# Group A attention: the products of a pair of query tiles issued in two halves, at other places of the TensorE order

## What is computed

```python
qa = _axial_rope(_rmsnorm(qa.reshape(b, s, N_Q_A, HEAD_DIM), q_norm_a[i]), tables)   # 8 query heads of 64
ka = _axial_rope(_rmsnorm(ka.reshape(b, s, N_KV_A, HEAD_DIM), k_norm_a[i]), tables)  # 2 key/value heads
sc = jnp.einsum('bqkgd,bskd->bkgqs', qblk, k) * scale      # scores of 128 queries against all keys
p = jax.nn.softmax(sc, axis=-1)
o = jnp.einsum('bkgqs,bskd->bqkgd', p, v)                  # "weighing" of the values
```

## Time and profile before

| | us |
|---|---|
| three runs, median | 2393.69 (2391.83 to 2396.62) |
| the profiled execution | 2396.31 |
| its span, first to last instruction | 2394.2 |
| outside the span | 2.1 |
| PE busy in the span | 2247.9 (94%) |
| DVE busy in the span | 1621.3 (68%) |
| ACT busy in the span | 802.1 (34%) |

### The profile page before, as it was taken

The page is one execution under the profiler, slowest core; times in us unless marked ns, Lnnn a source line. Parts: engine busy times, 40 slices in busy tenths (PEclk is TensorE's granted clock), DMA queues, the critical chain, the costliest instruction groups (busy, mean ns, idle before and its releaser), DMA issues.

```text
span 2394.2 us, 30366 instructions
## 1 busy us (share of the span) xinstructions
PE 2247.9 (94%) x11036; PEld 1842.2 (77%) x11036; DVE 1621.3 (68%) x2130; ACT 802.1 (34%) x1281; POOL 297.7 (12%) x184
## 2 busy tenths in 40 slices
PE   6999998888899998998999999999999999987996
PEld 4777876777777787777888888888888888876884
DVE  7677427777766664774777776777777776775545
ACT  5222107666755553132121221122211222134223
POOL 6101010000000000540000000000000000014100
PEclk9999999999999998998999999999999999997997
DMA  5223445101045523010110000000000100010102
GB/s 164 101 83 115 152 143 121 27 13 26 15 89 108 108 54 123 35 36 18 36 35 26 35 35 26 35 35 26 35 35 26 35 35 26 35 53 18 44 27 105
DMA packets 51020, 137.47 MB, mean 57 GB/s; under 512 B 20240, under 2 KB 20752, under 8 KB 50960
## 3 DMA queue, kind: packets, MB, share of 16 engines
q1 hardware_dynamic: 50096, 135.55, 18.7%
q10 hardware_dynamic: 864, 1.13, 0.1%
HBM read 105.99 MB, written 30.67 MB: 57 GB/s over the span
## 4 chain that ended last, share of the span: by engine, by line
PE 68%; issue 23%; DVE 4%; POOL 2%; ACT 1%; DMA 1%; SPq 0%; POOLq 0%; ACTq 0%; DVEq 0%
PE ps L297 22%; PE ps L298 22%; PE ps L299 22%; POOL acc_a L915 1%; DVE WL L293 1%; POOL acc_b L915 1%; DVE NL L629 1%; PE ps L485 1%; PE ps L480 1%; DVE NL L1733 1%; DMA raw<-in_w 0%; DVE NL L1414 0%; DVE H L1905 0%; DMA ident<-in_ident 0%; PE ps L1244 0%
## 5 line engine op out<-in xcount | busy, mean ns | idle before, releaser
L297 PE MATMUL ps<-NH,WH 128*128 128x512 f32 x1896 | 756.8, 399 | 44.3 <-DVE WL L293 30.8
L298 PE MATMUL ps<-NL,WH 128*128 128x512 f32 x1896 | 743.5, 392 | 0.0
L299 PE MATMUL ps<-NH,WL 128*128 128x512 f32 x1896 | 742.8, 392 | 0.0
L297 PEld LDWEIGHTS ps<-NH,WH 128*128 128x128 f32 x1896 | 359.6, 190 | 129.4 <-issue 36.2
L298 PEld LDWEIGHTS ps<-NL,WH 128*128 128x128 f32 x1896 | 359.5, 190 | 79.9 <-issue 6.0
L299 PEld LDWEIGHTS ps<-NH,WL 128*128 128x128 f32 x1896 | 359.1, 189 | 76.0
L1665 DVE TENSOR_TENSOR H<-H,ps 128x512 f32<-128x512 f32 x480 | 305.4, 682 | 106.6 <-PE ps L299 106.6
L274 POOL TENSOR_TENSOR raw<-raw,gains 128x1024 f32<-128x1024 f32 x78 | 156.3, 2009 | 1378.7 <-DMA raw<-in_w 1368.2
L289 ACT ACTIVATE WH<-raw 128x1024 fp32r<-128x1024 f32 x104 | 109.9, 1057 | 574.9 <-PE ps L299 548.8
L955 PE MATMUL ps<-ident,PR 128*128 128x128 f32 (+1 forms) x1056 | 164.5, 285 | 49.8 <-DVE PTL L1158 45.0
L297 PE MATMUL ps<-MH,WH 128*128 128x512 f32 x504 | 197.9, 393 | 4.7 <-DVE H L1740 4.5
(11 more groups left out here) (166 smaller groups left out, 2814.9 us busy)
## 6 DMA issues: line engine op xcount, KB each, us to landing
raw<-in_w SPq DMA_DIRECT2D x102, 512.0 KB, 3.2
xst<-in_xT SPq DMA_DIRECT2D x24, 256.0 KB, 4.3
H<-in_xT SPq DMA_DIRECT2D x8, 768.0 KB, 10.4
out_yT<-H SPq DMA_DIRECT2D x24, 256.0 KB, 2.1
qkh<-oqh SPq DMA_DIRECT2D x5, 768.0 KB, 3.3
qkl<-oql SPq DMA_DIRECT2D x5, 768.0 KB, 4.9
qkh<-obh SPq DMA_DIRECT2D x5, 768.0 KB, 3.5
qkl<-obl SPq DMA_DIRECT2D x5, 768.0 KB, 6.0
```

The source lines that it names most:

```text
L297: nc.tensor.matmul(out, wh, xh, start=first, stop=False)
L298: nc.tensor.matmul(out, wh, xl, start=False, stop=False)
L299: return nc.tensor.matmul(out, wl, xh, start=False, stop=last)
```

## The change

`weigh` gets an argument that selects a part of a pair's products. In group A an even step now weighs the first half of the pair `m - 2`, `m - 1`, behind the step's transposes, and the odd step that follows weighs the second half between its scores and its transposes. In an odd step the transposes thus come last. Steps 0 and 1 of the next pair of heads do the same for the last items of the pair before. Group B keeps its order. No instruction is added or removed, and the lists of ACT and DVE are the same.

```diff
-            def weigh(kind, p, b, m, queries):
+            def weigh(kind, p, b, m, queries, part=slice(None)):
...
-                for kb, kn, n in todo:
+                for kb, kn, n in todo[part]:
...
             def weigh_step(kind, p, m):
 
-                if kind == "A" and m % 2 == 1:
-                    mm = weigh(kind, p, (m - 3) // 4, m - 3, 2 * P)
+                if kind == "A":
+                    first = m - 2 - m % 2
+                    half = window(kind, first)[1] // P // 2
+                    mm = weigh(kind, p, first // 4, first, 2 * P, slice(half, None) if m % 2 else slice(half))
                     if m % 4 == 1:
                         mm.then_inc(pv_done, 1)
...
+                own = kind if m > 1 else before
+                early = own == "A" and m % 2 == 1
+                if i is not None and not early:
                     turn(kind, p, m)
-                if m >= 3 or kind == "B" and m == 2:
+                if m > 1:
                     weigh_step(kind, p, m)
-                elif m < 2 and before:
+                elif before:
                     weigh_step(before, p - 1, m + ITEMS)
+                if i is not None and early:
+                    turn(kind, p, m)
                 if i is not None and m % 4 == 3:
                     norm_row(p, m // 4)
```

## The result

| kernel | median us | ratio to the kernel before (95%) |
|---|---|---|
| before, beside it | 2396.62 (2391.83 to 2398.41) | |
| changed | 2416.03 (2407.51 to 2419.96) | 1.0075 (1.0060 to 1.0089) |

The change makes the kernel 19 us slower. The forecast was 2394 us, that is 0.4 us more than before, and the range ended at 2407.

What follows compares the result with a forecast made beforehand. The prediction took DVE to carry group A's loop, held by two waits. A 6.6 us loss from the order less 6.2 us back from the clock gave 0.4 us, added to the median 2393.69: 2394 us, range 2383 to 2407.

Steps and rivals of the forecast that it cites:

- DVE's two waits: Group A: DVE waits 35.6 us for scores and 24.7 us for ACT's copy `osum`, at most 60 us together.
- Norm halves: Steps 2 and 3 of group A's blocks: the wait for scores goes, later transposes replace it; 1.94 us a head gained.
- The moved wait for `o_done`: Second sample block's norm half: scores arrive before DVE needs them, so this wait costs nothing, with 0.1 us of slack.
- the wait for scores: Sign in the changed profile: DVE's wait for scores, 35.6 us before, should be about 8 us.
- The wait for `PTH`: New sign: DVE waits for `PTH` of odd steps, 0.4 to 1.3 us in five of a head's six halves.
- Output halves: Steps 0 and 1: later transposes delay `PTH`, and ACT does `osum` behind it and the next exponential; 2.77 us a head lost.
- The net of both: Group A: 2.77 us lost less 1.94 gained, 0.83 us a head lost, 6.6 us for eight heads.
- The squares on ACT: 0.6 us in three steps of a pair, given nothing because DVE has slack; without slack up to 7 us.
- The clock: Step 19 of each pair: four falls of 1.56 us disappear, since PE's wait becomes 2.05 us; 6.2 us back.
- The slower case, 2405 us: Later odd-step transposes take 0.87 us to `PTH`, and the clock still falls once a pair: 11.4 us slower; chance 0.25.
- The case with a fall in every block, 2431 us: Only transposes and waits precede each block's first product, so the clock falls in all 24 blocks: 37.8 us; chance 0.05.
- The row that the prediction set against that reason: Window 393.70 to 397.10, read as little but transposes (1.30 us) and waits, with the clock at 1.00 throughout.

Runs made afterwards that it cites:

- run 7: Kernel before, with step 2 making the scores of two items ahead of PE's wait and step 3 weighing the whole pair, then transposing: 2365.7 us.
- run 10: Kernel before, with two items' scores in step 2, output-half products split behind each step's transposes, and `osum` ahead of the exponential on ACT: 2352.54 us.
- run 4: Changed kernel, with scores of item `m + 3` made once more than needed ahead of the wait for `o_done`: 2391.62 us.
- run 6: Kernel before, with eight extra transposes of the identity filling PE's wait in step 3 of each block: 2389.6 us.
- run 3: Changed kernel, products still split over both steps, but the odd step's second half again behind its transposes: 2372.6 us.
- run 9: Changed kernel, with the copy `osum` moved ahead of the exponential of item `m+2` on ACT: 2373.16 us.
- run 12: Changed kernel again, unedited, for a second trace: 2410.78 us.
- run 5: Changed kernel, with eight extra transposes of the identity ahead of the wait for `o_done` in step 2 of each block: 2393.03 us.
- run 2: New order only in steps 0 and 1 of each block (output halves), norm halves as in the kernel before: 2436.98 us.
- run 1: New order only in steps 2 and 3 of each block (norm halves), output halves as in the kernel before: 2377.21 us.
- run 11: Changed kernel, with two extra transposes of the identity ahead of the wait for `o_done` in step 2 of each block: 2394.04 us.

## Why the prediction was wrong

**What bounded the kernel: right.** DVE's two waits carried the loop. Versions that take them away gain what was in them: runs 7 and 10.

**Norm halves: the mechanism and the sizes right, at full clock.** Predicted gain 1.94 us a head, measured 2.20 (runs 4 and 6). The moved wait for `o_done` cost nothing by itself, and the later transposes took the place of the late scores. Of the signs that the prediction named, the wait for scores, "about 8 us", is 7.1 at full clock. The wait for `PTH`, "some 38 us", is 28.4 there; that the changed kernel shows 37.7 is luck, since its falls lengthened that wait.

**Output halves: right.** Predicted loss 2.77 us a head, measured 2.44. It takes both causes that the prediction named. Without the moved transposes (run 3) the output halves are 5.54, 7.03 and 7.51 in place of 6.65, 7.51 and 8.43; and `osum` was held by ACT's order, since with that order changed (run 9) 0.85 us of each output half goes.

**The net of both: mis-sized.** 6.6 us was predicted for the order, 1.3 measured (290.9 against 289.6): six terms, each within 0.2 us, whose errors nearly all lay on one side. The squares on ACT, given nothing, cost nothing that could be seen.

**The clock: this step failed.** The prediction said that a wait of 2.05 us "is nearer to 2.43 than to 2.69, so I expect no fall, and 6.2 us back". The wait was 1.95 to 2.12 us, as computed. But of the 22 such waits 17 had a fall in one trace and 12 in another. In place of 6.2 us back, the four old falls gave back 6.0 and the new ones cost 26.3, so the clock made the kernel about 20 us slower. This alone puts the time out of the range. The step drew a line between two lengths of one wait, both seen only in the old order, and used it for a wait at another place of the order. The line was also drawn from one trace, and run 12 shows that one trace does not fix the number of falls.

The price of a fall was nearly right: 1.56 us predicted, 1.5 measured. The 1.56 compared two blocks that differ by themselves: at full clock (run 6) the one at which the clock fell takes 6.55 us and the other 6.42.

**The rivals.** The slower case, 2405 us, had the right direction and the wrong mechanism: it took the later transposes for the price and one fall a pair. Its condition for falls, "where it and the short waits before it come near 2.69 us", fits the block shown (2.00 with 0.49 and 0.18 before it, 2.67 together), but not all: with 2.12 and 0.23 before it the clock fell too, and with 2.00, 0.94 and 0.18, 3.12 together, it did not in the first trace. Its price was four falls in any case. The case with a fall in every block, 2431 us, had the right effect, many falls at about 1.5 us each, and was given 0.05; its reason, that transposes do not hold the clock, is refuted by run 5.

The row that the prediction set against that reason, was weak evidence. In all lines its window is

```profile
393.70:397.10 3.40, 1.77 (x14) 1.27 (x12) 3.10 (x6) 1.98 (x5) 0.00 (x0) 1.00 0.25 52
```

so 0.47 of the 1.77 us in which PE is busy are score products, and most of the rest is PE waiting. The stretch is not "made of little else" than transposes; only run 5 isolates them.

**What stays open.** Why one wait of 2.0 us has a fall and the next has not. Neither the longest wait nor the sum of neighbouring waits sorts the cases. In the old order the long waits of 1.79 to 2.45 us were passed without a fall. In the changed kernel the four blocks with the longest short wait ahead, 0.94 to 1.01 us, are just those that had no fall in the first trace, apart from the last of all, and two of the four had one in the second. Run 3 had no fall at waits of 1.83 to 1.95 us with almost no stand ahead, but its other waits are shorter too, and it has one trace. That PE's standing there is the cause is shown by runs 4, 5 and 6, each of which fills it and changes nothing else; the rule behind it is not shown.

## What to carry to other kernels

When a change moves a wait of TensorE, list all of its standing around the new place, short waits too, and price a fall of the clock at every repetition as a case of its own, since nothing in the old order says that it will hold. A few useful instructions moved into that wait (here the next item's scores), or even a quarter of a microsecond of work that nobody needs, can be worth more than the reordering itself. And before products are moved to make a result ready earlier, look at what its reader has queued ahead of the read: here one line on ACT was worth 17 us of read-out and 26 us of falls.

## What the runs showed of the hardware

- The granted clock fell from 2.4 to 1.2 GHz at stands of PE's load queue of 1.95 to 2.12 us in the changed kernel (17 of 22 in the first trace, 12 of 22 in the second). In the kernel before, stands of 1.79 to 2.45 us had no fall and the four of 2.64 to 2.69 us had one each; in run 2, stands of 2.8 to 3.3 us had one in 18 of 22 places. Each fall cost about 1.5 us, since the work behind it was what DVE waited for.
- The number and the places of the falls differed between executions of one program with the same waits: 17 and 12, at 2419.96 and 2407.88 us, of which 7.9 us lie in group A. The spread of the times alone does not show it: it is 12 us over five runs of the changed kernel, but also 11 us over the four runs of run 1, whose trace has no fall in group A.
- Transposes of the identity held the clock as well as products did: no fall with eight of them in each block (runs 5 and 6), three with two (run 11).
